# First two input tiles by fours of k in turn, on one Trainium2 core

## The reference

```python
def rmsnorm(x, w):
    return x * rsqrt(mean(x * x, axis=-1) + EPS) * w
a = rmsnorm(h, norm_mix_w)
z = a @ w_in
u_s5, z_pool, q, k, v, g_lr, r = split(z)
# S5: A_bar = exp((a_re + i a_im) * exp(log_dt)); B_bar = (A_bar - 1) / A * B; scan over tokens; C, skip, GLU
h = h + concat(s5, pool, gla) @ W_out
h = h + (silu(conv(gate)) * val) @ W_down      # gate, val = rmsnorm(h) @ W_up
h = h + (p @ W_ple) * sigmoid(rmsnorm(h) @ W_pg)
return rmsnorm(h) * final_norm_w
```

## Time and profile before

| | us |
|---|---|
| median of 3 runs | 2214.38 (2214.12 to 2214.69) |
| the profiled execution's own time | 2214.82 |
| its span | 2212.9 |
| PE busy | 2186.6 (99%) |
| DVE, ACT, POOL busy | 1390.4, 885.8, 310.3 |
| chain that ended last | PE 86%, POOL 7%, DVE 3% |

### The profile page before, as it was taken

The page is one execution under the profiler, slowest core; times in us unless marked ns, Lnnn a source line. Parts: engine busy times, 40 slices in busy tenths (PEclk is TensorE's granted clock), DMA queues, the critical chain, the costliest instruction groups (busy, mean ns, idle before and its releaser), DMA issues.

```text
span 2212.9 us, 28977 instructions
## 1 busy us (share of the span) xinstructions
PE 2186.6 (99%) x10892; PEld 1841.9 (83%) x10892; DVE 1390.4 (63%) x1731; ACT 885.8 (40%) x1000; POOL 310.3 (14%) x332
## 2 busy tenths in 40 slices
PE   9999999999999899999999999999999999999997
PEld 7888878878888788888888888888888888888886
DVE  7486236553367988888888888886333333446444
ACT  6222245442242544455444545443222121226333
POOL 6993005000000111111111111110000000000001
PEclk9999999999999999999999999999999999999999
DMA  6423222133333677777777777776343332233222
GB/s 219 133 74 106 95 92 82 57 119 141 144 109 119 196 209 200 191 201 209 207 204 207 193 191 206 212 204 235 98 140 105 122 123 94 91 114 113 95 95 76
DMA packets 106037, 322.05 MB, mean 146 GB/s; under 512 B 8224, under 2 KB 56992, under 8 KB 85632
## 3 DMA queue, kind: packets, MB, share of 16 engines
q1 hardware_dynamic: 76112, 268.39, 34.0%
q0 software_dynamic: 29872, 52.96, 13.1%
HBM read 299.30 MB, written 22.02 MB: 145 GB/s over the span
## 4 chain that ended last, share of the span: by engine, by line
PE 86%; POOL 7%; DVE 3%; DMA 1%; ACT 1%; issue 1%; SPq 0%; DVEq 0%; ACTq 0%; POOLq 0%
PE bank L989 22%; PE bank L674 17%; PE bank L676 17%; PE bank L675 17%; PE bank L991 12%; DVE w_lo L1926 1%; PE bank L776 1%; DMA Y<-in_x 1%; DMA w_raw<-in_w_up 1%; DVE xs_lo L1541 1%; POOL QKV L2253 0%; DVE x_block L1920 0%; POOL QKV L2273 0%; POOL Q L2294 0%; POOL Y L2289 0%
## 5 line engine op out<-in xcount | busy, mean ns | idle before, releaser
L989 PE MATMUL bank<-x_block,w_hi 128*128 128x512 f32 x2240 | 778.1, 391 | 5.8 <-DVE w_lo L1926 2.2
L991 PE MATMUL bank<-x_block,w_lo 128*128 128x256 f32 x2240 | 629.0, 281 | 0.0
L1071 ACT ACTIVATE w_hi<-w_raw 128x2048 fp32r<-128x2048 f32 (+1 forms) x134 | 222.5, 1661 | 741.3 <-PE bank L676 728.1
L989 PEld LDWEIGHTS bank<-x_block,w_hi 128*128 128x128 f32 x2240 | 419.6, 187 | 98.5 <-DVE w_lo L1926 5.1
L674 PE MATMUL bank<-xs_hi,w_hi 128*128 128x512 f32 x1152 | 456.2, 396 | 4.3 <-DVE xs_lo L1543 2.7
L676 PE MATMUL bank<-xs_hi,w_lo 128*128 128x512 f32 x1152 | 449.2, 390 | 0.0
L675 PE MATMUL bank<-xs_lo,w_hi 128*128 128x512 f32 x1152 | 449.0, 390 | 0.0
L991 PEld LDWEIGHTS bank<-x_block,w_lo 128*128 128x128 f32 x2240 | 423.3, 189 | 0.0
L1519 DVE TENSOR_TENSOR w_lo<-w_raw,w_hi 128x2048 fp32r<-128x2048 f32 (+1 forms) x136 | 271.8, 1999 | 105.9 <-ACT w_hi L1071 103.3
L674 PEld LDWEIGHTS bank<-xs_hi,w_hi 128*128 128x128 f32 x1152 | 216.6, 188 | 53.8 <-issue 5.7
L675 PEld LDWEIGHTS bank<-xs_lo,w_hi 128*128 128x128 f32 x1152 | 216.8, 188 | 46.7 <-issue 2.6
(11 more groups left out here) (342 smaller groups left out, 2319.9 us busy)
## 6 DMA issues: line engine op xcount, KB each, us to landing
w_raw<-in_w_up SPq DMA_DIRECT2D x48, 1024.0 KB, 5.0
w_raw<-in_w_down SPq DMA_DIRECT2D x64, 704.0 KB, 4.1
Y<-in_w_up SPq DMA_DIRECT2D x40, 1024.0 KB, 6.3
w_raw<-in_w_in SPq DMA_DIRECT2D x31, 1024.0 KB, 4.9
Y<-in_w_up POOLq DMA_DIRECT2D x59, 512.0 KB, 6.7
Y<-in_w_up SPq DMA_DIRECT2D x39, 512.0 KB, 7.7
w_raw<-in_w_out SPq DMA_DIRECT2D x16, 1024.0 KB, 5.1
w_raw<-in_w_pg SPq DMA_DIRECT2D x16, 1024.0 KB, 4.7
```

Of the source, the lines that this page charges most:

```text
L989: nc.tensor.matmul(place(c, b, 0, 2), w_h[:, ks], xb[b][:, k, :, :].rearrange("p e t -> p (e t)"), start=fresh and k == 0, stop=False, ski ...
L991: last = nc.tensor.matmul(place(c, b), w_l[:, ks], xb[b][:, k, 0, :], start=False, stop=k == HALF_K - 1, skip_group_check=True)
L1071: nc.scalar.activation(w_hi[c % 2][:, 0:width], w_raw[c % 2][:, 0:width], ACT.Copy).then_inc(hi_made, 1)
```

## The change

The first two tiles are no longer made one after the other: PE takes four k of tile 0, four of tile 1, the next four of tile 0, and so on, in two banks. x comes in six groups (k 4-7 in two), and quarters of both tiles' weights are sent and split between them. Tile 2's weights come and are split in two halves; the first is sent when two quarters of tile 0 are split, the second when all four are, and the seven small inputs lie between. Exp and Sin for S5 are made on ACT between the fourth and the fifth group of x. Tile 2 is split after the fourth square, tile 3 after the twelfth, tile 4 ahead of the root; the sum over partitions moves to k=3 of tile 3 and the spread to its k=8. Some semaphores are used twice, with counts raised to suit.

```diff
-X_GROUPS = [0, 2, 4, 8, 12, 16]
+X_GROUPS = [0, 2, 4, 6, 8, 12, 16]
 FIRST_CHUNKS = 4
+CHUNK_KT = KT // FIRST_CHUNKS
+WITH_GROUP = [[(0, 0)], [(1, 0)], [(0, 1)], [(1, 1)], [(0, 2), (1, 2)], [(0, 3), (1, 3)]]
+STEP_TRIG_AT = 3
+FIRST_ORDER = [(0, 0), (1, 0), (0, 1), (1, 1), (0, 2), (1, 2), (0, 3), (1, 3)]
...
+        w2_first_in, W2_FIRST = x_in[0], 32
+        w2_first_hi, w2_first_lo, W2_HALF = first_hi, first_lo, FIRST_CHUNKS
...
@@ SP @@
-                        if g < FIRST_CHUNKS:
-                            cs = slice(g * D // FIRST_CHUNKS, (g + 1) * D // FIRST_CHUNKS)
-                            sp.dma_start(w_raw[0][:, cs], src[:, cs]).then_inc(u_in[g], 16)
-                else:
-                    weights(n, 0, src, in_width(n), free=n >= 2)
-                if n == 1:
+                        for first, c in WITH_GROUP[g]:
+                            cs = slice(c * D // FIRST_CHUNKS, (c + 1) * D // FIRST_CHUNKS)
+                            sp.dma_start(w_raw[first][:, cs],
+                                         A["w_in"][first][:, cs]).then_inc((u_in, y_in)[first][c], 16)
+                elif n > 2:
+                    weights(n, 0, src, in_width(n))
+                if n == 2:
+                    sp.wait_ge(first_lo, FIRST_CHUNKS // 2)
+                    sp.dma_start(w_raw[0][:, 0:D // 2], src[:, 0:D // 2]).then_inc(w2_first_in, 16)
                     sp.dma_start(ident[:], A["ident"]).then_inc(s5_in, 16)
...
+                    sp.wait_ge(lo_made, 1)
+                    sp.dma_start(w_raw[0][:, D // 2:], src[:, D // 2:]).then_inc(w_in[0], 16)
...
@@ PE @@
+            for n, c in FIRST_ORDER:
+                pe.wait_ge(*((lo_made, n + 1) if c == FIRST_CHUNKS - 1 else ((first_lo, lo_begun)[n], c + 1)))
+                for k in range(c * CHUNK_KT, (c + 1) * CHUNK_KT):
+                    pe.wait_ge(xs_lo_made, k + 1)
+                    ks = slice(k * P, (k + 1) * P)
+                    last = product(bank[n][:], w_hi[n][:, ks], w_lo[n][:, ks], xs_hi[:, k, :], xs_lo[:, k, :],
+                                   k == 0, k == KT - 1)
+                if c == FIRST_CHUNKS - 1:
+                    last.then_inc(tile_done, 1)
...
-                    if n == 2 and k == 8:
+                    if n == 3 and k == 3:
                         pe.wait_ge(ones_set, 1)
                         sum_tokens(KT, [x_ss], bank[7], sum_spread)
-                    if n == 3 and k == 1:
+                    if n == 3 and k == 8:
                         spread(diag_made, 1, x_diag, bank[7], rstd_spread)
...
@@ ACT @@
+                for first, c in WITH_GROUP[g]:
+                    cs = slice(c * D // FIRST_CHUNKS, (c + 1) * D // FIRST_CHUNKS)
+                    act.wait_ge((u_in, y_in)[first][c], 16)
+                    half = nc.scalar.activation(w_hi[first][:, cs], w_raw[first][:, cs], ACT.Copy)
+                    half.then_inc(hi_made if c == FIRST_CHUNKS - 1 else (first_hi, hi_begun)[first], 1)
+                if g == STEP_TRIG_AT:
+                    act.wait_ge(exp_in, 1)
+                    nc.scalar.activation(s5s[:, 3, :], s5s[:, 1, :], ACT.Exp)
+                    nc.scalar.activation(s5s[:, 17, :], s5s[:, 1, :], ACT.Exp, scale=float(STEPS)).then_inc(size_made, 1)
+                    act.wait_ge(step_turns, 1)
+                    nc.scalar.activation(s5s[:, 9, :], s5s[:, 6, :], ACT.Sin, scale=SIN_SCALE)
+                    nc.scalar.activation(s5s[:, 10, :], s5s[:, 6, :], ACT.Sin, scale=math.pi).then_inc(step_trig, 1)
             for k in range(KT):
...
-                if k == KT // 2 - 1:
-                    w_half(2)
-            w_half(3)
+                if k == 3:
+                    act.wait_ge(w2_first_in, W2_FIRST)
+                    act.wait_ge(tile_done, 1)
+                    nc.scalar.activation(w_hi[0][:, 0:D // 2], w_raw[0][:, 0:D // 2], ACT.Copy).then_inc(w2_first_hi, 1)
+                    landed(act, 2)
+                    nc.scalar.activation(w_hi[0][:, D // 2:], w_raw[0][:, D // 2:], ACT.Copy).then_inc(hi_made, 1)
+                if k == 11:
+                    w_half(3)
+            w_half(4)
             root(0, norm4[:, 1, :], norm4[:, 0, :])
...
@@ DVE: the same order: quarters of both tiles, tile 2 in halves at k=3, w_rest(3) at k=11 @@
-            rms_small(bank[7], 1.0 / D, var_made, root_made, diag_made, 1, x_diag, between=lambda: w_rest(3))
+            rms_small(bank[7], 1.0 / D, var_made, root_made, diag_made, 1, x_diag)
+            w_rest(4)
             dve.wait_ge(rstd_made, 1)
```

More of the change, by code:

```diff
@@ L289, in build @@
         params_in = sem("params_in")
-        x_in = [sem(f"x_in{g}") for g in range(len(X_GROUPS) - 1)]
+        x_in = [sem(f"x_in{g}") for g in range(len(X_GROUPS) - 2)]
         s5_in = sem("s5_in")
@@ L398, in build @@
         s3_made = sem("s3_made")
-        s1_in, S1_FROM = y_in[2:4], 16 * PER_BATCH
+        s1_in, S1_FROM = y_in[2:4], 16 * (PER_BATCH + 1)
         s1_made = sem("s1_made")
@@ L430, in build @@
         written = sem("written")
+        x_in.append(written)
+        WRITTEN_FROM = 16
+        w2_first_in, W2_FIRST = x_in[0], 32
+        w2_first_hi, w2_first_lo, W2_HALF = first_hi, first_lo, FIRST_CHUNKS
         v_link = sem("vector_link")
@@ L476, in landed @@
         def landed(eng, c, e=0):
-            eng.wait_ge(w_in[c % 2], (e + (c + 1) // 2) * 16)
+            eng.wait_ge(w_in[c % 2], (e + c // 2) * 16)
         def in_width(n):
@@ L666, in _ @@
                 sp.dma_start(A["out"][:, j, :], Y[:, j, :]).then_inc(written, 16)
-            sp.wait_ge(written, 16 * KT)
+            sp.wait_ge(written, WRITTEN_FROM + 16 * KT)
         @block.tensor
@@ L872, in _ @@
                 nc.tensor.matmul(bank[6][:, 0:P], ones[:], ones[:], start=True, stop=True)
-            for n in range(IN_TILES):
-                if n:
-                    pe.wait_ge(*((lo_begun, 1) if n < 2 else (lo_made, n + 1)))
+            for n, c in FIRST_ORDER:
[7 more added lines that the diff above has]
+                    last.then_inc(tile_done, 1)
+            for n in range(2, IN_TILES):
+                pe.wait_ge(*((w2_first_lo, W2_HALF) if n == 2 else (lo_made, n + 1)))
                 if n >= 4:
@@ L1071, in w_half @@
                 nc.scalar.activation(w_hi[c % 2][:, 0:width], w_raw[c % 2][:, 0:width], ACT.Copy).then_inc(hi_made, 1)
[L1073 to L1078, removed]
             def w_half_rank():
@@ L1258, in _ @@
                     w_half_rank()
-                elif n < IN_TILES - 1:
+                elif 2 < n < IN_TILES - 1:
                     w_half(n + 2)
@@ L1520, in w_rest @@
                    ALU.subtract).then_inc(lo_made, 1)
[L1522 to L1527, removed]
             def w_rest_rank():
@@ L1645, in add_skip @@
             def add_skip(c):
-                dve.wait_ge(y_in[c], 64)
+                dve.wait_ge(y_in[c], 80)
                 stt(y_back[:, c, :], Y[:, c, :], par("d", c), y_back[:, c, :], ALU.mult, ALU.add).then_inc(y_added, 1)
@@ L1751, in _ @@
                     x_rest(k, 0, "mix")
[L1752 to L1758, removed]
+                for first, c in WITH_GROUP[g]:
+                    cs = slice(c * D // FIRST_CHUNKS, (c + 1) * D // FIRST_CHUNKS)
+                    last = c == FIRST_CHUNKS - 1
+                    dve.wait_ge(*((hi_made, first + 1) if last else ((first_hi, hi_begun)[first], c + 1)))
+                    tt(w_lo[first][:, cs], w_raw[first][:, cs], w_hi[first][:, cs].bitcast(F32),
+                       ALU.subtract).then_inc(lo_made if last else (first_lo, lo_begun)[first], 1)
             for k in range(KT):
@@ L1762, in _ @@
                 dve.wait_ge(sq_used, k + 1)
-                if k == KT // 2 - 1:
-                    w_rest(2)
+                if k == 3:
+                    dve.wait_ge(w2_first_hi, W2_HALF)
+                    tt(w_lo[0][:, 0:D // 2], w_raw[0][:, 0:D // 2], w_hi[0][:, 0:D // 2].bitcast(F32),
+                       ALU.subtract).then_inc(w2_first_lo, 1)
+                    dve.wait_ge(hi_made, 3)
+                    tt(w_lo[0][:, D // 2:], w_raw[0][:, D // 2:], w_hi[0][:, D // 2:].bitcast(F32),
+                       ALU.subtract).then_inc(lo_made, 1)
+                if k == 11:
+                    w_rest(3)
             dve.wait_ge(s5_in, 80)
             dve.wait_ge(sum_spread, 1)
-            rms_small(bank[7], 1.0 / D, var_made, root_made, diag_made, 1, x_diag, between=lambda: w_rest(3))
+            rms_small(bank[7], 1.0 / D, var_made, root_made, diag_made, 1, x_diag)
+            w_rest(4)
             dve.wait_ge(rstd_made, 1)
@@ L1812, in _ @@
                     w_rest_rank()
-                elif n < IN_TILES - 1 and s not in (4, 6) and n != SPLIT_SCAN_AT + 1:
+                elif 2 < n < IN_TILES - 1 and s not in (4, 6) and n != SPLIT_SCAN_AT + 1:
                     w_rest(n + 2)
```

7 lines of the change are left out of this document (1 added, 6 removed).

## The result

The changed kernel takes 2217.85 us (median of 20 runs, 2215.86 to 2220.12), the kernel before 2214.01 (20 runs): ratio 1.0017, 95% interval 1.0011 to 1.0023. It is slower by 3.8 us, where 2212.1 was forecast, and outside the range of 2209.9 to 2214.8. The profiled execution took 2219.17 with a span of 2216.3; the median span of the 20 runs is 2215.4.

The account below looks back on a forecast made before the run. PE, busy 99% of the span, bounds the kernel, with DMA feeding the start; tile 2's start -2.7, sums +0.7, Q -0.3 make -2.3, so 2212.1 us, range 2209.9 to 2214.8.

Parts of the forecast that it names:

- The first two tiles: Start of the kernel: alternating fours of k shorten PE's pause, so tile 2 starts 2.0 to 3.2 us earlier, taken 2.7.
- The pause at k=8: Third four of tile 0: a new PE pause of 1.2 or 2.1 us takes the place of the 2.8.
- rival B: Third four ready at 19.6, a clean handover needing ACT free at 15.1; 4 to 5 us won, chance 0.11.
- the fast end: Start of the kernel: DMA at 425 GB/s, x[4:6] landing at 11.2 and x[8:12] at 16.2.
- The third tile in two parts: Start of tile 2: halves of its weights are made just when due, 0.15 us of wait kept, second half's landing hidden.
- Sine and cosine earlier: POOL's work up to the first push moves 8 us earlier; PE's Q wait goes, overlap with DVE costs 0.3.
- The wait on Q: Later in the kernel: PE's 0.3 us wait on POOL's Q should go, -0.3 in the sum.
- bounds 0 and 1, taken 0.3: Tile 3: cost in us of POOL's products running beside w_rest(3) and DVE's last adds.
- I assume no slow clock: Pause at the third four: shorter than the one after which the clock fell, so no slow-clock time counted.
- the 0.7: Sums in tile 3: net loss of 0.4 us from late adds plus 0.3 for POOL.
- Rival D: Tile 3's start: w2's second half, or squares under POOL, late; landing 3 to 8 us late gives 2215 to 2220; chance 0.08.
- After tile 3 every wait is on PE's own progress or unchanged, so the shift lasts to the end: Rest of the kernel behind tile 3: the forecast shift of -2.3 us reaches the end in full.

Follow-up runs that it names:

- e1: Changed kernel with sine and cosine moved behind all six groups of x instead of behind the fourth; 2214.41 us, ratio 1.0006 to the kernel before.
- e4: Changed kernel with tile 2 split in one piece, its two transfers kept; 2217.74 us, ratio 1.0017 to the kernel before.
- e8: Changed kernel with POOL's six 512-element products of B_bar cut into twelve of 256; 2214.47 us, ratio 1.0001 to the kernel before.
- e2: Changed kernel with POOL's 512-element products held until all 16 squares are added, sine still early; 2213.74 us, ratio 1.0000 to the kernel before.
- e3: Changed kernel with 11 filler matmuls on ones ahead of the sums in tile 3; 2214.77 us, ratio 1.0004 to the kernel before.
- e5: Changed kernel with POOL held as in e2, root's table loaded early, spread at k=11, tiles 4 and 5 waiting for their own bank only; 2216.19 us.
- e9: Changed kernel with POOL's products halved, sums at k=6, spread at k=12, early root table, tiles 4 and 5 waiting for their own bank only; 2212.38 us.
- e7: Kernel before with only the early sine and cosine added, behind the fourth group of x; 2214.47 us, ratio 1.0002 to the kernel before.
- e12: Changed kernel with POOL's products halved as in e8, plus 5 filler matmuls on ones ahead of the sums; 2213.57 us, ratio 0.9995 to the kernel before.
- the repetition: The changed kernel run again unaltered, on the same chip as e5's successors e9 and e10; 2218.35 us, ratio 1.0018 to the kernel before.
- e6: Changed kernel with only PE's places moved, sums at k=9 and spread at k=15 of tile 3; 2217.18 us, ratio 1.0015 to the kernel before.
- e10: Changed kernel with POOL's products whole, sums at k=10, spread at k=15, early root table, tiles 4 and 5 waiting for their own bank only; 2216.79 us.

## Why the prediction was wrong

**The first two tiles: right in the main.** The pause at k=8 is there, each figure a little ahead of its range: ACT at x[8:12] at 16.42 (16.8 to 18.1 forecast), the pause 0.9 us (1.2 to 2.1), tile 2 at 31.64 (31.9 to 33.1). The sine is not its main cause, though: without it (e1) ACT begins at 16.00, when x[8:12] lands, and 0.6 us of pause are left. The prediction's own landing of 16.2 said as much; with the 4.0 us from there to w_lo of (0,2), ACT would have had to be free at 15.6 for a clean handover, and not at 15.1 as under rival B. Landings were ahead of the fast end: ACT began on x[4:6] at 10.86, where 11.2 was the earliest of the sum. The next activation began 1.29 us after the table load's start, as in the rows of before. 3.4 us were won where I took 2.7.

**The third tile in two parts: right.** w_hi[0] and w_lo[0] came when PE wanted them, 0.03 us late, and the second half landed in time. What the halves win was lost further on (e4).

**Sine and cosine earlier: the step that failed.** The wait on Q did go. But of POOL's products beside w_rest(3) and the last adds the prediction said: "bounds 0 and 1, taken 0.3". They cost 0.85 us on w_lo and 3.2 on the adds, so that PE's wait at the sums, forecast at 0.6 us and 0.3 for POOL, was 4.0. I had one row for the overlap, a single long w_lo that lost 0.55, and applied it to a chain of four short adds that each wait for the one before. The row gives the price of one meeting; the adds have four. POOL's 1.05 to 1.3 us per product stood in its timeline, and four meetings of that kind bound the cost at some 4 to 5 us (an estimate from those rows; 3.2 was measured). The rule of the Trainium skill named under e8 (SBUF — State Buffer) would have led there. With the same POOL work held until the adds are over (e2), or cut in halves (e8), the adds take 2.9 and 4.3 us in place of 6.1.

**The clock: the second term left out.** "I assume no slow clock" was said of the pause at k=8, and held. For the wait at the sums, which my own sum had at 0.5 to 1 us, no slow clock was counted; at 4.0 us it came and cost 3.0 more (e3). With 4.0 - 0.26 for the wait, 3.0 for the clock and 0.15 for w_lo of tile 3 in place of the 0.7, the sum is -3.4 + 6.9 = +3.5 at the mark. That is an account of one and the same trace; what tests it are e2 and e3.

**Rival D was this case**, a late chain behind the squares under POOL with 2215 to 2220 us, at 0.08 far too low. It put the point of loss at 2.3 us late, and it lay at the sums rather than at the start of tile 3; its 2215 to 2220 was worked out for a late landing of w2's second half, which was in time, so that its number fits is in part luck. The margin for it was in the text ("the chain has no room for 0.5 us"), and a chain without room deserved a wider bound than 1 us.

**Behind tile 3.** "After tile 3 every wait is on PE's own progress or unchanged, so the shift lasts to the end" holds for the loss that came, but not for a gain: e5 and e9 were 4 us ahead at the mark and lost 2.8 of it to POOL's Q.

**The rest of the sum.** The span grew by 3.2 us in the median (2215.4 against 2212.2 of the 33 runs of before that were timed beside e1 to e4), the time by 3.8. The remaining 0.6 stands outside the span: time less span is 1.9 to 2.0 in each of those runs of before, but 1.9 to 3.8 in those of the changed kernel, 12 of 20 above 2.1. e3 and e7 have 1.9 to 2.0 throughout, e12 1.7 to 1.8. Its cause was not found.

## What to carry to other kernels

Before work of POOL is moved earlier, look at what DVE does in the stretch where it will then run: a chain of short DVE instructions, each waiting for the one before, can wait for one POOL instruction per link. Its price is bounded by the number of links times POOL's instruction (here 0.8 us a link beside products of 1.05 to 1.3), and shorter POOL instructions (e8) or another moment (e1, e2) lower or avoid it. A chain with no slack is priced with PE's clock: waits of PE of 1.5 and 4.0 us cost 0.9 and 3.0 us more than themselves here (e12, e3), and a few matmuls on ones in the wait took that away. What is won at the start is kept only if the next bound (here DVE's adds, then the diagonal, then POOL's Q) has room for it; check each in turn before the gain is counted.

## What was not expected of the hardware

With pauses of 2.1 us (e4), 1.5 (e8), 2.2 (e7), 3.2 (the repetition), 3.4 (e6) and 2.8 (e5) the granted clock went to 0.50 for some 3 to 7 us; with 1.9 (e2), 1.4 (e1), 2.3 (e10) and 2.8 (e9) it stayed at 1.00. So the length of the pause alone does not decide in this range, and runs of one kernel may differ by it: the 20 spans of the changed kernel lie between 2214.0 and 2216.6. That this is the reason for their spread was not shown.

The last store of the output takes 0.6 us longer to land in the changed kernel. DMA issues in the last 4 us (KB each, us to landing), of the kernel before and then of the changed one:

```profile
out_h<-Y SPq DMA_DIRECT2D x1, 256.0 KB, 3.0
```

```profile
out_h<-Y SPq DMA_DIRECT2D x1, 256.0 KB, 3.6
```

The median of the last two stores is 3.4 us in e1, e2, e3, e8 and e12 and 3.0 in e7, so it goes with the changed kernel's program, though no edit touches that part but the count that SP waits for. It is 0.6 of the span, and its cause stays open. The last store is issued 2.8 us later than before (2212.39 for 2209.55), so of the 3.5 us at the mark some 0.7 are made up before the end: 0.3 is PE's wait on Q that is gone, the rest was not traced.
